# Gated weights and diagonal matrices of a mixture-of-experts sum made on ACT instead of DVE

## What is computed

```python
expert = jnp.take_along_axis(ids, pos, axis=-1)       # 8 heads x 16 experts for a token
g = jax.nn.softmax(top_s, axis=-1)
u_sel = peer_u[expert]
a = jax.nn.gelu(jnp.einsum('bqhkd,bqd->bqhk', u_sel, hb))
v_sel = peer_v[expert]
return jnp.einsum('bqhk,bqhkd->bqd', g * a, v_sel)
```

## Time and profile before

| | us |
|---|---|
| three runs | 2064.85, 2057.81, 2064.69 |
| median of them | 2064.69 |
| the profiled execution, its own time | 2061.91 |
| its span, first to last instruction | 2060.1 |

### The profile page before, as it was taken

The page is one execution under the profiler, slowest core; times in us unless marked ns, Lnnn a source line. Parts: engine busy times, 40 slices in busy tenths (PEclk is TensorE's granted clock), DMA queues, the critical chain, the costliest instruction groups (busy, mean ns, idle before and its releaser), DMA issues.

```text
span 2060.1 us, 25356 instructions
## 1 busy us (share of the span) xinstructions
PE 1746.9 (85%) x9904; PEld 1349.1 (65%) x9904; DVE 1265.4 (61%) x2226; ACT 601.0 (29%) x899; POOL 433.6 (21%) x344
## 2 busy tenths in 40 slices
PE   5996898668787877866689669999999999999997
PEld 2984794335554545543333227999879996689997
DVE  2674366288788786766867575564525645665554
ACT  3434342211111110000000016754434443245442
POOL 1550461033333334333334310000000000000000
PEclk7998798689998998888899779999999999999999
DMA  7446638989999999999899961445425452153542
GB/s 327 154 186 273 262 128 376 426 359 387 397 353 381 367 389 379 387 406 387 350 411 403 403 248 69 178 166 189 158 82 202 170 202 82 47 199 130 198 147 100
DMA packets 57570, 538.51 MB, mean 261 GB/s; under 512 B 6384, under 2 KB 6512, under 8 KB 7152
## 3 DMA queue, kind: packets, MB, share of 16 engines
q1 hardware_dynamic: 20592, 268.48, 33.4%
q0 software_dynamic: 36864, 268.45, 32.7%
HBM read 535.86 MB, written 1.05 MB: 261 GB/s over the span
## 4 chain that ended last, share of the span: by engine, by line
PE 60%; DMA 22%; DVE 8%; issue 6%; POOL 2%; ACT 1%; POOLq 0%; DVEq 0%; another core or an unknown queue 0%; SPq 0%; ACTq 0%
PE psum L396 60%; DMA arena<-in_experts,idx_stage 17%; DMA ring<-in_w_ada 3%; POOL arena L895 1%; DVE arena L1598 1%; DMA ring<-in_w_in 1%; DVE rstd L1258 1%; DVE small L1597 1%; DVE small L1595 0%; DVE arena L1587 0%; DVE h_t L1292 0%; ACT upper L924 0%; DVE small L1587 0%; DVE h_t L1272 0%; DVE h_t L1270 0%
## 5 line engine op out<-in xcount | busy, mean ns | idle before, releaser
L396 PE MATMUL psum<-arena,small 128*128 128x512 f32 x560 | 322.2, 708 | 204.2 <-DVE small L1597 204.0
L1587 DVE CUSTOM_DVE_ANT_0 arena<-arena 128x1024 f32<-128x1024 f32 x256 | 313.7, 1225 | 239.3 <-DMA arena<-in_experts,idx_stage 179.4
L1231 DVE TENSOR_TENSOR ring_r<-ring,ring_r 128x1024 fp32r<-128x1024 f32 (+1 forms) x240 | 287.7, 1207 | 277.1 <-ACT ring_r L924 276.0
L396 PE MATMUL psum<-small_r,ring_r 128*128 128x256 f32 x2304 | 417.0, 281 | 9.4 <-DVE h_t_r L1298 9.4
L895 POOL DMA_INDIRECT arena<-in_experts,idx_stage x256 | 297.5, 1162 | 410.1 <-PE psum L396 333.8
L396 PEld LDWEIGHTS psum<-small_r,ring_r 128*128 128x128 f32 x2304 | 361.8, 189 | 11.2 <-issue 10.5
L396 PEld LDWEIGHTS psum<-arena,small 128*128 128x128 f32 x560 | 114.3, 216 | 356.2 <-DVE small L1597 250.6
L396 PE MATMUL psum<-h_t_r,ring_r 128*128 128x256 f32 x1152 | 329.9, 286 | 0.0
L396 PE MATMUL psum<-arena_r,ring_r 128*128 128x256 f32 x2208 | 326.3, 281 | 2.8 <-DVE arena_r L1280 2.8
L924 ACT ACTIVATE ring_r<-ring 128x1024 fp32r<-128x1024 f32 (+1 forms) x240 | 248.7, 1042 | 217.0 <-PE psum L396 213.8
L396 PEld LDWEIGHTS psum<-arena_r,ring_r 128*128 128x128 f32 x2208 | 290.6, 189 | 3.3 <-DVE arena_r L1280 3.2
(11 more groups left out here) (210 smaller groups left out, 1509.2 us busy)
## 6 DMA issues: line engine op xcount, KB each, us to landing
ring<-in_w_ffn SPq DMA_DIRECT2D x33, 2048.0 KB, 7.8
ring<-in_w_in SPq DMA_DIRECT2D x31, 2048.0 KB, 7.5
ring<-in_w_ada SPq DMA_DIRECT2D x30, 2048.0 KB, 10.7
ring<-in_w_ffn SPq DMA_DIRECT2D x24, 1408.0 KB, 6.3
ring<-in_w_out SPq DMA_DIRECT2D x4, 2048.0 KB, 8.1
ring<-in_peer_wq SPq DMA_DIRECT2D x4, 2048.0 KB, 7.4
ring<-in_p_ret SPq DMA_DIRECT2D x4, 2048.0 KB, 7.6
arena<-in_experts,idx_stage POOLq DMA_INDIRECT x256, 10.2
```

The source lines that it names most:

```text
L396: return nc.tensor.matmul(o, a, b, start=first, stop=last)
L1231: nc.vector.tensor_tensor(whole(i, ring_r), whole(i, ring), upper(i).bitcast(F32), ALU.subtract).then_inc(lo_made, 1)
L1587: step(nc.vector.tensor_tensor_reduce(u, u, h2[:, n // PER_TILE, :], 1.0, 0.0, ALU.mult, ALU.add, dots[:, n % 8, s:s + 1]), sem("dots"))
```

## The change

ACT makes the weights and the diagonal matrix of a batch, directly behind its gelu. It first waits for the gates of the tile (a count on L1532 of before), then makes the odd place's weight and the even place's weight by one activation each (Identity, the input a gate, the scale the gelu's value; semaphore `weights`), waits for these, waits that PE has finished with the diagonal matrix of batch n - 4, and makes the new one (Identity of the identity matrix, the scale the even weight). DVE's `sum_batch(n)` now begins by waiting for the odd weight and goes straight on to the odd place's sum.

```diff
+            def gate_and_diagonal(n):
+                gate = best.rearrange("p t h n -> p (t h n)")
+                act.wait_ge(sem("gates"), n // PER_TILE + 1)
+                act.wait_ge(sem("gelus"), n + 1)
+                for s in (1, 0):
+                    nc.scalar.activation(weights[:, n % 8, s:s + 1], gate[:, BATCH * n + s:BATCH * n + s + 1], ACT.Identity,
+                                         scale=acts[:, n % 8, s:s + 1]).then_inc(sem("weights"), 1)
+                act.wait_ge(sem("weights"), BATCH * (n + 1))
+                act.wait_ge(sem("row_free_pe"), n + 1)
+                nc.scalar.activation(diag[:, n % (GBUF // 2), :], ident, ACT.Identity,
+                                     scale=weights[:, n % 8, 0:1]).then_inc(sem("diag"), 1)
...
                 nc.scalar.activation(acts[:, n % 8, :], dots[:, n % 8, :], ACT.Gelu_apprx_tanh).then_inc(sem("gelus"), 1)
+                gate_and_diagonal(n)
...
-                step(TT(best[:, t], best[:, t], hsum[:, 0:8].unsqueeze(2).to_broadcast([P, PH, PSEL]), ALU.mult))
+                step(TT(best[:, t], best[:, t], hsum[:, 0:8].unsqueeze(2).to_broadcast([P, PH, PSEL]), ALU.mult), sem("gates"))
...
-                v.wait_ge(sem("gelus"), n + 1)
-                gate = flat(best[:, t])[:, b * BATCH:(b + 1) * BATCH]
-                step(TT(weights[:, n % 8, :], acts[:, n % 8, :], gate, ALU.mult))
-                v.wait_ge(sem("row_free_pe"), n + 1)
-                TS(diag[:, n % (GBUF // 2), :], ident, weights[:, n % 8, 0:1], None, ALU.mult).then_inc(sem("diag"), 1)
+                v.wait_ge(sem("weights"), BATCH * n + 1)
                 STT(y_of[t], rows[(BATCH * n + 1) % GBUF][:, D:2 * D], weights[:, n % 8, 1:2], y_of[t],
                     ALU.mult, ALU.add).then_inc(sem("row_free_dve"), 1)
```

## The result

The changed kernel takes **2002.3 us** in the median of four runs (1998.6 to 2003.9) against 2064.0 of the kernel before (2057.8 to 2064.9): a ratio of 0.970, 95% interval 0.968 to 0.972, 62 us less. The forecast was 2031 with a range from 2004 to 2054. The direction held, and so did the reason for it, the matrix's place in the order; the size did not. The rival "all comes back", 2003 us at a chance of 0.12, is what happened.

What follows compares the result with a forecast made beforehand. The prediction took gathers delayed by a closed ring of waits to bound the loop, losing 67 us. Recovery by stretches, 31 plus 2 less 1, gave 32 us: 2030 or 2033 by baseline, so 2031, range 2004 to 2054.

Steps and rivals of the forecast that it cites:

- all comes back: Rival for the expert loop: 2.6 us more slack absorbs nearly every disturbance; gain 60 us, 2003 us; chance 0.12.
- The stage and the floor: Loop from 441 to 1214 us: 298.14 MB at 422 GB/s take 706 us; it takes 773, so 67 are lost.
- The mechanism: In the loop, the diagonal matrix's price is its place behind the next batch's dots; moving it forward gains 4.3 us undisturbed.
- DVE's two instructions: In the loop, DVE loses two instructions a batch, 48 us of its time; by itself cover for gather waits, not gain.
- ACT's three: In the loop, ACT gains three activations a batch; matrix ready 1.2 us after the dots, 109 us more work, hidden.
- The places: Eight gather buffer places in the loop: each held 2.6 to 4.3 us less of 19.9, a gather more in hand.
- the sum: Loop's recovered time by stretches: 17.5 + 9 + 3 + 2 = 31, plus 2, less 1: 32 of 67 us.
- the gate rival: In the loop, ACT works in order, so batches caught behind context SiLUs delay PE and DVE: 2087 to 2110 us; chance 0.07.
- DMA at its bound: Rival: the loop's low rates are slow transfers, only idle 4% can be won; gain 10 us, 2053; chance 0.20.
- The HBM figure of about 358 GB/s: Skill's bound on loads from HBM: the loop would take 833 us and nothing could be won; the trace was to decide.
- No table is loaded for the new activations: Rival: Identity needs another table, 2 x 1.28 us before each diagonal matrix on ACT; instruction lists say no; chance 0.01.
- Signs that were set: Loop 30 us shorter at 402 GB/s, 835 us behind unchanged, PE's matrix wait under 80, DVE's gather wait above 120.

Runs made afterwards that it cites:

- dve_early: Kernel before, with DVE itself making weights and diagonal matrix of batch n ahead of the dots of batch n + 1; 2009.6 us, ratio 0.972.
- diag_batch_later: Changed kernel, with ACT waiting for the dots of batch n + 1 before making the diagonal matrix of batch n; 2059.0 us, ratio 0.997.
- half_sum_before: Kernel before, with PE's sum of the even places cut to one of two banks in all but a tile's first and last batches; 2034.1 us, ratio 0.987.
- the bare ring: Kernel before, with the choice ahead of the loop, most context matmuls left out and POOL's copy out of the way; 2099.7 us, holding the choice.
- the half sum: Changed kernel, with the sum of the even places on PE cut to one of two banks in most batches; 1998.1 us, ratio 0.968.

## Why the prediction was wrong in size and right in kind

- **The stage and the floor** held. 298.14 MB at 422 GB/s were given as 706 us, the loss as 67. The changed kernel has 296 MB in 719 us, 412 GB/s, and nothing that frees a place sooner brought it beyond 416 in the stretch from 500 to 1100 us.
- **The mechanism** held: the price is the matrix's place in the order. dve_early and diag_batch_later show it from both sides.
- **DVE's two instructions** were taken as cover, not gain: they were worth 5 us. DVE's busy time in the loop fell by 43 us, not 54: the two instructions overlap what follows them, as the 48 us of the same passage say.
- **ACT's three** were costed at 1.2 us to the matrix and measure 1.2; the matrix takes 402 ns where 390 was given, the weights 287 ns where 281 was.
- **The places** were to be held 2.6 to 4.3 us less; it was 4.7 on average, and the gathers' median time in hand grew by 3.1.
- **The step that failed** is in the sum: "Between them I go by stretches: half of the 35 us beside the choice, because DVE's pieces of several us are longer than the 2.6 us won; half of 8 and 10 where PE's chunks stand in the way". That gave 31 us; the loop gave 54. By stretches, at the prediction's own measure, the largest term went wrong most: half of the 35 us lost between 500 and 860 us was to come back, 17.5, and at 416 GB/s only 5 are still lost there, so 30 came back. The loss was laid to DVE's pieces of several us, each weighed against the 2.6 us won, once. But the pieces alone were worth about 9 of the 35 us, and half_sum_before shows the loss paid in nearly every turn: 0.9 us off PE's step was worth 30 us. Where each of some 32 turns pays, a lead of 2.6 us is 83 us, more than the 67 that were to be had, and so nearly all came back. The statement under "All comes back", that the ring had just enough at the undisturbed pace, fits the 15.1 to 15.4 us of the bare ring against 14.9. That rival was right in its reason as well as in its time; its chance of 0.12 was too low.
- **Small slips that change nothing**: the gate rival's terms, 35 and 17.5 us on 2062, add up to 2114 and not 2110; and the kernel before was not above 358 GB/s "throughout", since the earlier trace rows have 333 in the hole near 1000 us.
- **The rivals.** DMA at its bound (2053) fell: the rate went to 412 GB/s with more gathers in hand, so the low rates were not slow transfers. The HBM figure of about 358 GB/s of the Trainium skill ("DMA: Bandwidth & Descriptors", "Where 436 GB/s comes from") is passed by 412 over a whole loop here, so the measurement decides against it for this pattern. ACT as the gate fell: ACT waits 518 us for dots, and the waits of the changed kernel's loop name none of DVE for a weight. No table is loaded for the new activations, as the instruction lists said; the Trainium skill ("ScalarE: Activation LUTs", "Table sets: the hidden batching unit") agrees.
- **Signs that were set**: the 835 us and the clock of 0.98 behind the loop, DVE's wait for gathers over 120 us, and POOL's wait moving to L1608 came as written. The rate went to 412, not 402. PE's wait for the matrix, now made by ACT, fell to 141 us only and not under 80. With the loop at the pace of the transfers that wait costs nothing: halving PE's sum there was worth 4 us.

## What to carry to other kernels

In a ring of buffers, follow the chain of waits from one transfer to the next that it releases, count how many places it moves on, and hold its length against that number times the transfer time. Add what regularly stands ahead of a step on its engine, such as other work of PE or a copy. Where the chain is as long or longer, every turn pays for what comes in between, and a us taken off any step is worth up to a us times the number of turns until the ring has slack; beyond that it is worth next to nothing. What is needed only to give a buffer back belongs directly behind its inputs, not behind the wait for the next transfer; which engine makes it mattered by 7 us here.

## What the runs showed of the hardware

Taking 125 us of matmuls out of 600 lowered TensorE's granted clock from 0.89 to 0.76, between its levels of 1.2 and 2.4 GHz, and stretched the multiplications that were left from 709 to 841 ns; a lighter PE gave no time back in the kernel before. The gathers of 8 KB rows together with the slabs' loads came to 414 GB/s over 600 us in the changed kernel and 416 with the half sum, of 422 in the best stretches. In the kernel before they moved about 355 GB/s while two gathers were in hand and 380 with three, and 414 or more with four to six.
